# First projection fed from columns of x: one load per pair of k blocks, row statistics behind the key product

## Chip, cores, metric

One core of a Trainium2 chip. The metric is the device time of one execution in microseconds (us), median over runs. One profiled execution stands beside them: its own time, and the span from its first to its last instruction.

## The reference, cut to what matters

Three transformer layers over x (256 rows, 1024 features, float32), each a mixer and a feed-forward net, each behind an rms norm. The change touches the first norm and what is projected from it:

```python
def rmsnorm(x, g):
    y = xf * lax.rsqrt(jnp.mean(xf * xf, axis=-1, keepdims=True) + EPS)
    return (y * g.astype(jnp.float32)).astype(x.dtype)
...
n = rmsnorm(h, g_mix[layer])            # layer 0: h = x
proj = n @ w_in                          # 1024 features -> index queries, keys, q, k, v, gates ...
...
h = h + mixer_ab(n, ...)                 # x again, as rows, for the residual
```

## The kernel before

Every product is made from float32 split into two parts of the fp32r type, "hi" and "lo", as three products: hi·hi, hi·lo, lo·hi. All weights come as one stream of 156 tiles (128 partitions by up to 2048 columns), through three slots of `raw`, `whi`, `wlo` (L450 to L452). SyncE (SP) issues the loads in order, `stage(i)` at L2604; it waits until the lo part of tile i−3 is made. ScalarE (ACT) makes `whi` (`hi`, L1246), VectorE (DVE) makes `wlo` (`lo`, L1864), GpSimd (POOL) does so for parts of a few tiles. All engines run their instructions in the order written out by hand in `tensor_program`, `scalar_program`, `vector_program`, `sync_program`; an instruction that waits holds up all behind it. The eight PSUM banks go round in an order written in `plan_banks` (L269): a product waits until the last user of its bank has read it out.

Start of the kernel. x is loaded as rows, into `h`, in four pieces; between them tile 0 in two pieces (L2617 to L2623), then tiles 1 and 2, constants, the other vectors. TensorE (PE) runs warm-up products (`keep_warm`, L798), turns x by 16 transposes (`half_turn`, L699), and multiplies it with tiles 0 and 1 (`first_proj`, L809: per block k of 128 features and half of the rows three products of 512 columns, 48 in all). ACT reads the transposes out times the gain (`evac_turn`, L1257, hi part), DVE makes the lo part (L1874). The normalising factor of a row is not put in before the products; it is applied when a product is read out. It comes from `row_stats` (L1270): ACT squares the rows and takes exp(−ln/2) of their mean. As a row over all partitions, `RSB`, it is made by two more transposes ("rowf", L846 to L850).

Then, in PE's order: `rowf`, the key product (tile 2, L852 to L856), the first product of tile 3 (L882, "qkb 0") with `key_turn` between its halves, tile 4 ("qkb 1") with `index_turn`, `scores(0, 4)` (L892), and `proj(1)` with tiles 5 and 6. ACT's order behind the first tiles: `row_stats`, hi(2), hi(3), the read-out of the first projection (L1318 to L1321), of `rowf` (L1324), hi(4), hi(5), the keys' read-out (L1327), hi(6). DVE's: lo(2), lo(3), the keys times `RSB` (L1924), lo(4), lo(5), `rope` (L1888), `branch(0)` (L1927), running sums, `level_diff`, lo(6), `branch(1)`, which reads qkb 1 out of its bank. The first bank of `proj(1)` is the one that held qkb 1 (`plan_banks`, by counting).

Of the kernel before, what the change touches and what calls it, by code (L numbers as in the profile page):

```python
# [8 lines left out]
ALU = mybir.AluOpType  # L9
ACT = mybir.ActivationFunctionType  # L10
# [4 lines left out]
P = 128  # L15
# [11 lines left out]
NSLOT = 3  # L27
AHEAD = 2
# [6 lines left out]
    ("gq_row", 128), ("gk_row", 128), ("g_mix0", 8), ("eps", 1),  # L35
# [233 lines left out]
def plan_banks(banks):  # L269
# [135 lines left out]
def block_kernel(nc, W, V, C, DL, CM, TRI, X, MT, WG, GP, OUT):  # L405
    ctx = ExitStack()
    with ctx:
# [98 lines left out]
        o_id = VEC["g_mix0"][0]  # L506
        o_masks = CST["inval"][0]
        GAIN = ["g_mix0", "g_ffn0", "g_mix1", "g_ffn1", "g_mix_pre"]
# [32 lines left out]
        QKE = A(8 * 512).rearrange("p (l n) -> p l n", l=8)  # L541
# [75 lines left out]
        s_w, s_i, s_v, s_c, s_r, s_o, s_g, s_d, s_gp = (sem("s_" + n) for n in ("w", "i", "v", "c", "r", "o", "g", "d", "gp"))  # L617
        s_x = [[sem(f"s_x{tt}{c}") for c in range(2)] for tt in range(2)]
# [7 lines left out]
        s_nhi, s_nlo = sig("nhi", grid(5, 8)), sig("nlo", grid(5, 4))  # L626
        s_un, s_nc, s_nchi, s_nclo = (sig(n, range(4)) for n in ("un", "nc", "nchi", "nclo"))
        s_uhi, s_ulo = sig("uhi", range(8)), sig("ulo", range(8))
        s_stat = sig("stat", grid(5, 3))
# [28 lines left out]
        def n_ready(t, k):  # L658

            if k % 2 == 0:  # L660
                return s_nlo.at(t, k // 2)
            return use["tr", t, k // 2].gone() if t < 4 else s_nodd.at(k // 2)

        def h_ready(t):

            if t == 0:
                return [[(s_x[tt][c], 16) for c in range(2)] for tt in range(2)]
            return [[use["out", t - 1, 2 * tt + c].gone() for c in range(2)] for tt in range(2)]
# [7 lines left out]
        def tensor_program(pe):  # L676
# [128 lines left out]
            keep_warm(use["tr", 0, 2].t, AM[:, 0:P], AM[:, 0:256], 4)  # L805
            half_turn(0, 0)
            keep_warm(use["tr", 0, 2].t, AM[:, 0:P], AM[:, 0:256], 3)

            def first_proj():  # L809
                us = [begin("pj", 0, 0), begin("pj", 0, 1)]  # L810
                w = [weights(i, 4) for i in range(2)]

                def high(k, tt):
                    on.wait_ge(*s_nhi.at(0, k))
                    on.wait_ge(*s_hi01.at(k // 4, k % 4))
                    pe.matmul(us[tt].t[:, :], nTa[:, k, tt * P:tt * P + P].hi, w[k // 4][:, k % 4, :].hi, start=k == 0, stop=False)  # L816

                def low_rows(k, tt):
                    on.wait_ge(*n_ready(0, k))
                    pe.matmul(us[tt].t[:, :], nTa[:, k, tt * P:tt * P + P].lo, w[k // 4][:, k % 4, :].hi, start=False, stop=False)  # L820

                def low_weights(k, tt):
                    weights_in(k // 4, k % 4)
                    return pe.matmul(us[tt].t[:, :], nTa[:, k, tt * P:tt * P + P].hi, w[k // 4][:, k % 4, :].lo, start=False, stop=k == 7)  # L824

                for k, tt in product(range(2), range(2)):
# [24 lines left out]

# [387 lines left out]
        def scalar_program(act):  # L1239
# [30 lines left out]
            def row_stats(t):  # L1270
# [7 lines left out]
                on.wait_ge(*TV)  # L1278
# [581 lines left out]
        def vector_program(dve):  # L1860
# [12 lines left out]

            def evac_turn(t, q, dst):  # L1874
# [47 lines left out]
            on.wait_ge(*use["rowf",].gone())  # L1922
# [677 lines left out]

        def sync_program(sp):
# [132 lines left out]
def vectors(a):  # L2734
# [53 lines left out]
```

## Time and profile before

| | us |
|---|---|
| median of 3 runs | 959.68 |
| lowest, highest | 959.44, 959.92 |
| the profiled execution's own time | 959.49 |
| its span | 957.5 |
| PE busy in the span | 948.9 (99%) |
| DVE, ACT busy | 613.1 (64%), 547.3 (57%) |

A start in the profile is counted from the span's start. Queues of an engine (SPq, ACTq) are its DMA issues. Consecutive like instructions are merged in the timeline: "2.20 ... x4" is four in 2.20 us.

### The profile page before, as it was taken

What the parts mean: (1) busy time and instruction counts of PE and PEld (TensorE: products, weight loads), DVE (VectorE), ACT (ScalarE), POOL (GpSimd) and SP (SyncE); (2) the same over time, 40 slices, a digit from 0 to 9 for tenths busy, and PEclk for the clock granted to TensorE, in tenths of its full rate; (3) what the DMA queues carried; (4) which work ended last, traced back from release to release, by engine and by line L of the source; (5) the groups of instructions that cost most, each with busy time, mean ns of one, the idle gap of its engine ahead of it and who ended that gap; (6) DMA issues with size and microseconds to landing.
All of it is one profiled execution on the core that took longest, in us unless ns stands there. A gap on an engine that the chain in (4) does not pass through costs nothing.

```text
span 957.5 us, 14406 instructions
## 1 busy us (share of the span) xinstructions
PE 948.9 (99%) x5992; PEld 842.8 (88%) x5992; DVE 613.1 (64%) x890; ACT 547.3 (57%) x781; POOL 134.6 (14%) x44
## 2 busy tenths in 40 slices
PE   9999999999999999999999999999999999999997
PEld 7888888888888888888888888899999999999886
DVE  5997847777222667747777522486558699888643
ACT  7676547666333558847666333635465687665442
POOL 0021250000664000020000665300000000000000
PEclk9999999999999999999999999999999999999999
DMA  8554245554555452435544555364444535554541
GB/s 307 214 186 161 90 138 183 204 180 176 201 194 203 156 214 88 177 140 183 204 180 176 196 200 180 140 220 177 156 157 163 185 155 184 207 182 177 187 166 44
DMA packets 25344, 168.21 MB, mean 176 GB/s; under 512 B 2816, under 2 KB 3904, under 8 KB 5568
## 3 DMA queue, kind: packets, MB, share of 16 engines
q1 hardware_dynamic: 25136, 167.23, 48.5%
q8 instruction: 47, 0.77, 0.3%
q14 instruction: 17, 0.14, 0.0%
q10 hardware_dynamic: 144, 0.07, 0.0%
HBM read 166.24 MB, written 1.05 MB: 175 GB/s over the span
## 4 chain that ended last, share of the span: by engine, by line
PE 95%; ACT 2%; DVE 2%; issue 0%; POOL 0%; DVEq 0%; ACTq 0%; POOLq 0%
PE bank L680 23%; PE bank L681 23%; PE bank L682 23%; PE bank L762 12%; PE bank L766 6%; PE bank L708 1%; PE bank L800 1%; DVE wlo L1867 0%; PE bank L900 0%; PE bank L816 0%; PE bank L1030 0%; PE bank L1164 0%; ACT whi L1251 0%; PE bank L824 0%; PE bank L820 0%
## 5 line engine op out<-in xcount | busy, mean ns | idle before, releaser
L1867 DVE TENSOR_TENSOR wlo<-raw,whi 128x2048 fp32r<-128x2048 f32 (+2 forms) x151 | 309.4, 2049 | 249.9 <-ACT whi L1251 249.9
L1251 ACT ACTIVATE whi<-raw 128x2048 fp32r<-128x2048 f32 (+1 forms) x154 | 293.4, 1906 | 151.7 <-PE bank L682 149.9
L2597 POOL TENSOR_TENSOR wlo<-raw,whi 128x1024 fp32r<-128x1024 f32 (+1 forms) x38 | 133.1, 3504 | 473.2 <-ACT whi L1251 465.8
L762 PE MATMUL bank<-nhl,whi 128*128 128x512 f32 x512 | 124.2, 392 | 0.0
L762 PEld LDWEIGHTS bank<-nhl,whi 128*128 128x128 f32 x512 | 93.9, 188 | 19.1 <-issue 0.7
L680 PE MATMUL bank<-mhi,whi 128*128 128x258 f32 x384 | 108.6, 283 | 0.0
L681 PE MATMUL bank<-mlo,whi 128*128 128x258 f32 x384 | 108.3, 282 | 0.0
L682 PE MATMUL bank<-mhi,wlo 128*128 128x258 f32 x384 | 108.2, 282 | 0.0
L680 PE MATMUL bank<-nhl,whi 128*128 128x258 f32 (+3 forms) x320 | 92.3, 288 | 0.8 <-DVE wlo L1867 0.8
L681 PE MATMUL bank<-nhl,whi 128*128 128x258 f32 (+3 forms) x320 | 91.4, 286 | 0.0
L682 PE MATMUL bank<-nhl,wlo 128*128 128x258 f32 (+3 forms) x320 | 90.5, 283 | 0.0
L682 PEld LDWEIGHTS bank<-mhi,wlo 128*128 128x128 f32 x384 | 72.7, 189 | 0.0
L680 PEld LDWEIGHTS bank<-mhi,whi 128*128 128x128 f32 x384 | 72.6, 189 | 0.1
L681 PEld LDWEIGHTS bank<-mlo,whi 128*128 128x128 f32 x384 | 72.6, 189 | 0.0
L680 PE MATMUL bank<-whi,nhl 128*128 128x512 f32 x176 | 70.4, 400 | 0.0
L682 PE MATMUL bank<-whi,nhl 128*128 128x512 f32 x176 | 68.7, 390 | 0.0
L681 PE MATMUL bank<-wlo,nhl 128*128 128x512 f32 x176 | 68.5, 389 | 0.0
L766 PEld LDWEIGHTS bank<-nhl,wlo 128*128 128x128 f32 x512 | 66.2, 191 | 2.5
L766 PE MATMUL bank<-nhl,wlo 128*128 128x256 f32 x512 | 67.7, 283 | 0.0
L680 PEld LDWEIGHTS bank<-nhl,whi 128*128 128x128 f32 (+1 forms) x320 | 60.5, 189 | 1.7 <-DVE wlo L1867 1.0
L681 PEld LDWEIGHTS bank<-nhl,whi 128*128 128x128 f32 (+1 forms) x320 | 60.0, 188 | 0.1
L682 PEld LDWEIGHTS bank<-nhl,wlo 128*128 128x128 f32 (+1 forms) x320 | 60.1, 188 | 0.0
(329 smaller groups left out, 1741.8 us busy)
## 6 DMA issues: line engine op xcount, KB each, us to landing
raw<-w_stream SPq DMA_DIRECT2D x154, 1024.0 KB, 4.8
h<-x_rows SPq DMA_DIRECT2D x4, 256.0 KB, 4.6
raw<-w_stream SPq DMA_DIRECT2D x2, 512.0 KB, 5.6
cst<-consts SPq DMA_DIRECT2D x1, 832.0 KB, 6.4
out_rows<-e SPq DMA_DIRECT2D x3, 256.0 KB, 2.0
e<-g_post SPq DMA_DIRECT2D x1, 512.0 KB, 3.3
raw<-w_stream SPq DMA_DIRECT2D x1, 352.0 KB, 9.1
vec<-vectors SPq DMA_DIRECT2D x1, 258.5 KB, 8.5
```

The lines of the kernel that those rows point to most:

```text
L680: pe.matmul(out, lhsT.hi, rhs.hi, start=start, stop=False)
L681: pe.matmul(out, lhsT.hi, rhs.lo, start=False, stop=False)
L682: return pe.matmul(out, lhsT.lo, rhs.hi, start=False, stop=stop)
L708: x = pe.transpose(u.t[:, kk * 256 + tt * P:kk * 256 + tt * P + P], h[:, tt, k * P:k * P + P], ident)
L762: return pe.matmul(us[c].t[:, :], w[:, k, c * P:c * P + P].hi, nboth[:, k, :], start=k == 0, stop=k == 7)
L766: pe.matmul(us[c].t[:, 0:256], w[:, k, c * P:c * P + P].lo, nTa[:, k, :].hi, start=False, stop=False)
L800: pe.matmul(t[:, 0:256], lhsT, rhs, start=True, stop=True)
L1251: act.activation(whi[j][:, 0:n], raw[j][:, 0:n], ACT.Copy).then_inc(s_hi.up(i))
L1867: dve.tensor_tensor(wlo[j][:, 0:m], raw[j][:, 0:m], whi[j][:, 0:m].bitcast(F32), ALU.subtract).then_inc(s_lod.up(i))
L2597: pool.tensor_tensor(wlo[j][:, m:n], raw[j][:, m:n], whi[j][:, m:n].bitcast(F32), ALU.subtract).then_inc(s_lop.up(i))
```

## The change

Columns of x (features on partitions) come as a new input, `x_cols`, with the first gain as eight columns in front. They are loaded in six parts, each beside the weights of the same k blocks; the first part's weights are issued by ACT, the rest by SP. No transposes of x are made in the first layer; ACT and DVE split the loaded columns directly, and PE's first product runs k by k. The squares are made in place by ACT, summed over k by DVE in three additions, and over partitions by PE with a matrix of ones, behind the key product; from there ACT takes both forms of the factor. The rows of x are loaded before tile 11. The diff is cut to its core.

```diff
+FIRST_PARTS = [(0, 1), (1, 2), (2, 3), (3, 4), (4, 6), (6, 8)]
@@ plan_banks
-    for q in range(4):
-        banks.take("tr", 0, q)
     proj(0)
-    banks.take("rowf")
     banks.take("keys")
     last[KEYS] = (("keys",), 0)
+    banks.take("rowf")
@@ block_kernel
+        xc = qke[:, 0:8 + 8 * S]
+        g_first, XT = xc[:, 0:8], xc[:, 8:8 + 8 * S].rearrange("p (k t) -> p k t", k=8)
+        s_wc = [sem("s_wc0"), sem("s_wc1"), sem("s_wc2"), s_raw[0], sem("s_wc4"), s_raw[1]]
@@ tensor_program
-            keep_warm(use["tr", 0, 2].t, AM[:, 0:P], AM[:, 0:256], 4)
-            half_turn(0, 0)
-            keep_warm(use["tr", 0, 2].t, AM[:, 0:P], AM[:, 0:256], 3)
+            keep_warm(use["rowf",].t, AM[:, 0:P], AM[:, 0:256], 4)
...
-                for k, tt in product(range(2), range(2)):
-                    high(k, tt)
-                half_turn(0, 1)
-                for part in (low_rows, low_weights):
-                    for k, tt in product(range(2), range(2)):
-                        part(k, tt)
-                for k in range(2, 5):
+                for k in range(5):
                     for part in (high, low_rows, low_weights):
                         for tt in range(2):
                             x = part(k, tt)
...
-            u = begin("rowf")
-            on.wait_ge(*s_stat.at(0, 1))
-            for tt in range(2):
-                x = pe.transpose(u.t[:, tt * P:tt * P + P], bc(stats[0][2][:, tt:tt + 1], [P, P]), ident)
-            x.then_inc(u.full)
             w, u = weights(KEYS, 8), begin("keys")
...
+            u = begin("rowf")
+            on.wait_ge(*TC)
+            on.wait_ge(*s_xss.at(2))
+            pe.matmul(u.t[:, 0:256], ones, XT[:, 0, :], start=True, stop=True)
+            for tt in range(2):
+                x = pe.matmul(u.t[:, 256 + tt:257 + tt], XT[:, 0, tt * P:tt * P + P], ones[:, 0:1], start=True, stop=True)
+            x.then_inc(u.full)
             def key_turn():
                 u = begin("keyT")
+                on.wait_ge(*TI)
@@ scalar_program
             def hi01(i, c):
-                on.wait_ge(*((s_w, 16) if i == 0 and c >= 2 else (s_raw[i], 16)))
+                on.wait_ge(s_wc[part_of(4 * i + c)], 16)
...
+            def first_hi(k):
+                on.wait_ge(s_xc[0], 16)
+                on.wait_ge(s_xc[part_of(k)], 16)
+                act.activation(nTa[:, k, :].hi, XT[:, k, :], ACT.Copy, scale=g_first[:, k:k + 1]).then_inc(s_xhi.up(k))
+            def first_squares(j):
+                x = XT[:, 2 * j:2 * j + 2, :]
+                on.wait_ge(*s_xlo.at(2 * j + 1))
+                act.activation(x, x, ACT.Square).then_inc(s_xsq.up(j))
+            def first_stats():
+                ss, lnrs, rs, rs2 = stats[0]
+                u = use["rowf",]
+                on.wait_ge(*TI)
+                on.wait_ge(*u.done())
+                act.activation(ss, u.t[:, 256:258], ACT.Ln, bias=eps, scale=1.0 / D).then_inc(own.up())
+                act.activation(RSB, u.t[:, 0:256], ACT.Ln, bias=eps, scale=1.0 / D).then_inc(u.free)
+                on.wait_ge(*own.last())
+                act.activation(lnrs, ss, ACT.Copy, scale=-0.5).then_inc(s_stat.up(0, 0))
+                act.activation(rs, ss, ACT.Exp, scale=-0.5).then_inc(s_stat.up(0, 1))
+                on.wait_ge(*u.gone())
+                act.activation(RSB, RSB, ACT.Exp, scale=-0.5).then_inc(s_rsb.up(0))
...
-            evac_turn(0, 0, nTa)
-            hi01(0, 0)
-            hi01(0, 1)
-            evac_turn(0, 1, nTa)
...
-            hi01(1, 3)
-            row_stats(0)
-            rs = stats[0][2]
-            on.wait_ge(*s_stat.at(0, 2))
+            for k in range(8):
+                if k:
+                    first_hi(k)
+                hi01(k // 4, k % 4)
+                if k in (4, 5):
+                    first_squares(k - 4)
+            first_squares(2)
+            first_squares(3)
             hi(2)
             hi(3)
+            first_stats()
+            rs = stats[0][2]
+            on.wait_ge(*s_stat.at(0, 1))
             for tt in range(2):
                 u = use["pj", 0, tt]
                 on.wait_ge(*u.done(1))
                 act.activation(IQ[:, tt * 576:tt * 576 + 512], u.t[:, :], ACT.Copy, scale=rs[:, tt:tt + 1]).then_inc(u.free)
-            u = use["rowf",]
-            on.wait_ge(*u.done())
-            act.activation(RSB, u.t[:, 0:256], ACT.Copy).then_inc(u.free)
             hi(4)
             hi(5)
@@ vector_program
+            def first_lo(k):
+                o = nTa[:, k, :]
+                on.wait_ge(*(s_xhi.at(k) if k else s_xhi0.at(0)))
+                dve.scalar_tensor_tensor(out=o.lo, in0=XT[:, k, :], scalar=g_first[:, k:k + 1], in1=o.hi.bitcast(F32),
+                                         op0=ALU.mult, op1=ALU.subtract).then_inc(s_xlo.up(k))
...
-            evac_turn(0, 0, nTa)
-            lo01(0, 0)
-            lo01(0, 1)
-            evac_turn(0, 1, nTa)
...
-            lo01(1, 3)
+            on.wait_ge(s_xc[0], 16)
+            dve.tensor_scalar(nTa[:, 0, :].hi, XT[:, 0, :], g_first[:, 0:1], None, ALU.mult).then_inc(s_xhi0.up(0))
+            for k in range(8):
+                first_lo(k)
+                lo01(k // 4, k % 4)
+            for j, half in enumerate((4, 2, 1)):
+                a = XT[:, 0:half, :]
+                on.wait_ge(*(s_xss.at(j - 1) if j else s_xsq.at(3)))
+                dve.tensor_tensor(a, a, XT[:, half:2 * half, :], ALU.add).then_inc(s_xss.up(j))
             lo(2)
             lo(3)
             u = use["keys",]
-            on.wait_ge(*use["rowf",].gone())
+            on.wait_ge(*s_rsb.at(0))
@@ add_out (residual, first mixer)
+                if s == 0:
+                    on.wait_ge(s_x[tt], 16)
@@ sync_program
+        def first_weights(eng, n):
+            a, b = FIRST_PARTS[n]
+            i, s = a // 4, slice(a % 4 * 512, a % 4 * 512 + (b - a) * 512)
+            src = W[starts[i]:starts[i + 1]].rearrange("(p n) -> p n", p=P)
+            eng.dma_start(raw[i][:, s], src[:, s]).then_inc(s_wc[n], 16)
...
-            first = W[0:starts[1]].rearrange("(p n) -> p n", p=P)
-            for c in range(2):
-                for tt in range(2):
-                    sp.dma_start(h[:, tt, c * 512:c * 512 + 512], X[tt * P:tt * P + P, c * 512:c * 512 + 512]).then_inc(s_x[tt][c], 16)
-                sp.dma_start(raw[0][:, c * 1024:c * 1024 + 1024], first[:, c * 1024:c * 1024 + 1024]).then_inc(s_w if c else s_raw[0], 16)
-            for i in range(1, NSLOT):
-                stage(i)
+            for n, (a, b) in enumerate(FIRST_PARTS):
+                s = slice(8 + a * S if a else 0, 8 + b * S)
+                sp.dma_start(xc[:, s], XC[:, s]).then_inc(s_xc[n], 16)
+                if n:
+                    first_weights(sp, n)
+            sp.dma_start(vec[:, o_id:NVEC], V[:, o_id:NVEC]).then_inc(s_i, 16)
             sp.dma_start(cst[:, 0:o_masks], C[:, 0:o_masks]).then_inc(s_c, 16)
+            stage(2)
+            stage(3)
             sp.dma_start(wg, WG).then_inc(s_c, 16)
             sp.dma_start(vec[:, 0:o_id], V[:, 0:o_id]).then_inc(s_v, 16)
-            for i in range(NSLOT, NTILE):
+            for i in range(NSLOT + 1, NTILE):
+                if i == NSLOT + 8:
+                    for tt in range(2):
+                        sp.dma_start(h[:, tt, :], X[tt * P:tt * P + P, :]).then_inc(s_x[tt], 16)
@@ @block.scalar
-            eng.dma_start(vec[:, o_id:NVEC], V[:, o_id:NVEC]).then_inc(s_i, 16)
+            first_weights(eng, 0)
```

The removed calls of ACT and DVE are those of L1301 to L1312 and L1906 to L1917. `TC` is there when both `cst` and `wg` have landed. The factor exp(−ln) and its wait (L1283, L1289) are left out for the first layer. The constants' layout loses the column block of the first gain.

## Rows read from the trace of the kernel before

**Rows 1.** Page, part 4: shares of the chain that ended last.

```profile
PE 95%; ACT 2%; DVE 2%; issue 0%; POOL 0%; DVEq 0%; ACTq 0%; POOLq 0%
```

**Rows 2.** Waits of PE, whole kernel: us in total, times, longest.

```profile
PE bank L800 <- POOL a L2585: 1.3, 1, 1.3
PE bank L680 <- DVE wlo L1867: 0.8, 1, 0.8
```

**Rows 3.** Timeline of PE: start, us, line, operation, count.

```profile
1.31 3.78 PE L800 MATMUL bank<-a 128*128 128x256 f32 x8 [1.31 <-POOL a L2585]
...
7.49 1.22 PE L816 MATMUL bank<-whi,nhl 128*128 128x512 f32 x4
...
15.36 0.39 PE L816 MATMUL bank<-whi,nhl 128*128 128x512 f32 x1
...
19.21 0.39 PE L824 MATMUL bank<-wlo,nhl 128*128 128x512 f32 x1
...
19.57 0.36 PE L680 MATMUL bank<-nhl,whi 128*88 128x256 f32 x1
...
22.48 0.28 PE L680 MATMUL bank<-nhl,whi 128*128 128x256 f32 x1
...
25.60 1.13 PE L866 MATMUL bank<-a,a 64*128 64x256 f32 x4
...
38.60 0.50 PE L680 MATMUL bank<-whi,nhl 128*128 128x512 f32 x1
```

**Rows 4.** DMA issues at 0.73, 3.06 and 3.53 us: KB, us to landing.

```profile
h<-x_rows SPq DMA_DIRECT2D x1, 256.0 KB, 3.2
raw<-w_stream SPq DMA_DIRECT2D x1, 512.0 KB, 6.4
raw<-w_stream SPq DMA_DIRECT2D x1, 1024.0 KB, 8.5
```

**Rows 5.** Stretches: busy us by engine, granted clock, DMA share, GB/s.

```profile
2.00:3.00 1.00, 1.00 (x4) 0.82 (x3) 0.00 (x0) 0.47 (x1) 0.00 (x0) 1.00 0.70 218
3.00:7.00 4.00, 4.00 (x18) 3.34 (x18) 0.14 (x1) 1.01 (x3) 0.00 (x0) 1.00 0.96 306
8.00:11.00 3.00, 3.00 (x18) 2.60 (x18) 2.45 (x6) 2.20 (x6) 0.00 (x0) 1.00 1.04 433
```

**Rows 6.** Timeline of ACT.

```profile
12.02 2.20 ACT L1255 ACTIVATE whi<-raw 128x512 fp32r<-128x512 f32 x4
...
16.33 0.29 ACT L1279 ACTIVATE rows<-rows,vec 128x2 f32<-128x2 f32 x1
...
17.08 2.60 ACT L1251 ACTIVATE whi<-raw 128x704 fp32r<-128x704 f32 x2
19.58 1.25 ACT L1321 ACTIVATE a<-bank,rows 128x512 f32<-128x512 f32 x2
20.72 0.38 ACT L1324 ACTIVATE a<-bank 128x256 f32<-128x256 f32 x1
20.98 1.92 ACT L1251 ACTIVATE whi<-raw 128x2048 fp32r<-128x2048 f32 x1
...
65.06 1.90 ACT L1251 ACTIVATE whi<-raw 128x2048 fp32r<-128x2048 f32 x1
```

**Rows 7.** Timeline of DVE.

```profile
17.90 0.89 DVE L1867 TENSOR_TENSOR wlo<-raw,whi 128x704 fp32r<-128x704 f32 x1 [2.36 <-ACT whi L1251]
...
26.29 2.29 DVE L1867 TENSOR_TENSOR wlo<-raw,whi 128x2048 fp32r<-128x2048 f32 x1 [0.92 <-ACT whi L1251]
...
33.10 0.42 DVE L1963 TENSOR_TENSOR a<-a 128x256 f32<-128x256 f32 x1
...
36.68 0.69 DVE L1930 SCALAR_TENSOR_TENSOR a<-bank,a 128x512 f32<-128x512 f32 x1
...
50.92 2.28 DVE L1867 TENSOR_TENSOR wlo<-raw,whi 128x2048 fp32r<-128x2048 f32 x1
...
122.97 1.23 DVE L1867 TENSOR_TENSOR wlo<-raw,whi 128x1024 fp32r<-128x1024 f32 x1 [0.39 <-ACT whi L1251]
```

More of the change, by code:

```diff
@@ L34 @@
     ("conv_b_mix", 4), ("g_mix_post", 8), ("g_ffn_pre", 8), ("conv_w_ffn", 132), ("conv_b_ffn", 44),
-    ("gq_row", 128), ("gk_row", 128), ("g_mix0", 8), ("eps", 1),
+    ("gq_row", 128), ("gk_row", 128), ("eps", 1),
     ("ident", 128),
@@ L402, in plan_banks, with block_kernel @@
     return last
-def block_kernel(nc, W, V, C, DL, CM, TRI, X, MT, WG, GP, OUT):
+def block_kernel(nc, W, V, C, DL, CM, TRI, X, XC, MT, WG, GP, OUT):
     ctx = ExitStack()
@@ L505, in block_kernel @@
         ones = const("ones")
-        o_id = VEC["g_mix0"][0]
+        o_id = VEC["eps"][0]
         o_masks = CST["inval"][0]
-        GAIN = ["g_mix0", "g_ffn0", "g_mix1", "g_ffn1", "g_mix_pre"]
+        GAIN = [None, "g_ffn0", "g_mix1", "g_ffn1", "g_mix_pre"]
         stats = [[rows[:, 8 * t + 2 * i:8 * t + 2 * i + 2] for i in range(4)] for t in range(5)]
@@ L540, in block_kernel @@
         QA = xn.rearrange("p t (h d) -> p t h d", h=8)
-        QKE = A(8 * 512).rearrange("p (l n) -> p l n", l=8)
+        qke = A(8 * 512)
+        QKE = qke.rearrange("p (l n) -> p l n", l=8)
+        xc = qke[:, 0:8 + 8 * S]
+        g_first, XT = xc[:, 0:8], xc[:, 8:8 + 8 * S].rearrange("p (k t) -> p k t", k=8)
         IW = small[:, 16:32]
@@ L616, in block_kernel @@
         s_raw = [sem(f"raw{i}") for i in range(NSLOT)]
-        s_w, s_i, s_v, s_c, s_r, s_o, s_g, s_d, s_gp = (sem("s_" + n) for n in ("w", "i", "v", "c", "r", "o", "g", "d", "gp"))
-        s_x = [[sem(f"s_x{tt}{c}") for c in range(2)] for tt in range(2)]
+        s_i, s_v, s_c, s_r, s_o, s_g, s_d, s_gp = (sem("s_" + n) for n in ("i", "v", "c", "r", "o", "g", "d", "gp"))
+        s_x = [sem(f"s_x{tt}") for tt in range(2)]
+        s_xc = [sem(f"s_xc{n}") for n in range(len(FIRST_PARTS))]
+        s_wc = [sem("s_wc0"), sem("s_wc1"), sem("s_wc2"), s_raw[0], sem("s_wc4"), s_raw[1]]
         TI, TV, TC, TR, TM, TD, TGP = (s_i, 16), (s_v, 16), (s_c, 32), (s_r, 32), (s_g, 16), (s_d, 32), (s_gp, 16)
@@ L625, in block_kernel @@
         s_lop = sig("lop", [i for i in range(2, NTILE) if cuts[i] < sizes[i]])
-        s_nhi, s_nlo = sig("nhi", grid(5, 8)), sig("nlo", grid(5, 4))
+        s_xhi0, s_xhi, s_xlo = sig("xhi0", [0]), sig("xhi", range(1, 8)), sig("xlo", range(8))
+        s_nhi, s_nlo = sig("nhi", [(t, k) for t in range(1, 5) for k in range(8)]), sig("nlo", [(t, q) for t in range(1, 5) for q in range(4)])
         s_un, s_nc, s_nchi, s_nclo = (sig(n, range(4)) for n in ("un", "nc", "nchi", "nclo"))
         s_uhi, s_ulo = sig("uhi", range(8)), sig("ulo", range(8))
-        s_stat = sig("stat", grid(5, 3))
+        s_stat = sig("stat", grid(5, 3)[:2] + grid(5, 3)[3:])
+        s_xsq, s_xss = sig("xsq", range(4)), sig("xss", range(3))
         s_dg, s_rsb, s_gl, s_iq, s_key = sig("dg", range(2)), sig("rsb", [0]), sig("gl", [0]), sig("iq", range(2)), sig("key", range(2))
@@ L658, in n_ready @@
         def n_ready(t, k):
+            if t == 0:
+                return s_xlo.at(k)
             if k % 2 == 0:
@@ L662, in n_ready, with part_of @@
             return use["tr", t, k // 2].gone() if t < 4 else s_nodd.at(k // 2)
+        def part_of(k):
+            return next(n for n, (a, b) in enumerate(FIRST_PARTS) if a <= k < b)
         def h_ready(t):
-            if t == 0:
-                return [[(s_x[tt][c], 16) for c in range(2)] for tt in range(2)]
             return [[use["out", t - 1, 2 * tt + c].gone() for c in range(2)] for tt in range(2)]
@@ L813, in high @@
                 def high(k, tt):
-                    on.wait_ge(*s_nhi.at(0, k))
+                    on.wait_ge(*(s_xhi.at(k) if k else s_xhi0.at(0)))
                     on.wait_ge(*s_hi01.at(k // 4, k % 4))
@@ L1253, in hi01 @@
             def hi01(i, c):
-                on.wait_ge(*((s_w, 16) if i == 0 and c >= 2 else (s_raw[i], 16)))
+                on.wait_ge(s_wc[part_of(4 * i + c)], 16)
                 act.activation(whi[i][:, c * 512:c * 512 + 512], raw[i][:, c * 512:c * 512 + 512], ACT.Copy).then_inc(s_hi01.up(i, c))
+            def first_hi(k):
[18 more added lines that the diff above has]
+                act.activation(RSB, RSB, ACT.Exp, scale=-0.5).then_inc(s_rsb.up(0))
             def evac_turn(t, q, dst):
                 u = use["tr", t, q]
-                on.wait_ge(*(TI if t == 0 else TV))
+                on.wait_ge(*TV)
                 on.wait_ge(*u.done())
@@ L1277, in row_stats @@
                 on.wait_ge(*own.last())
-                on.wait_ge(*TV)
+                on.wait_ge(*TI)
                 act.activation(ss, ss, ACT.Ln, bias=eps, scale=1.0 / D).then_inc(own.up())
@@ L1288, in inv_rms_row @@
                 on.wait_ge(*own.last())
-                on.wait_ge(*s_stat.at(t, 2))
                 act.activation(ss, ss, ACT.Exp, bias=stats[t][1][:, tt:tt + 1], scale=-0.5).then_inc(done)
@@ L1872, in lo01 @@
                 dve.tensor_tensor(wlo[i][:, s], raw[i][:, s], whi[i][:, s].bitcast(F32), ALU.subtract).then_inc(s_lo01.up(i, c))
+            def first_lo(k):
+                o = nTa[:, k, :]
+                on.wait_ge(*(s_xhi.at(k) if k else s_xhi0.at(0)))
+                dve.scalar_tensor_tensor(out=o.lo, in0=XT[:, k, :], scalar=g_first[:, k:k + 1], in1=o.hi.bitcast(F32),
+                                         op0=ALU.mult, op1=ALU.subtract).then_inc(s_xlo.up(k))
             def evac_turn(t, q, dst):
@@ L2739, in put @@
         v[:, o:o + n] = np.asarray(x).reshape(-1, P).T
+    put("g_mix1", a["g_mix"][1])
     for l in range(2):
-        put(f"g_mix{l}", a["g_mix"][l])
         put(f"g_ffn{l}", a["g_ffn"][l])
@@ L2769 @@
     c, dlx, cm, tri = constants()
+    x_cols = a["x"][0].T.reshape(8, P, S).transpose(1, 0, 2).reshape(P, 8 * S)
     arrays = {
@@ L2777 @@
         "x_rows": np.ascontiguousarray(a["x"][0]),
+        "x_cols": np.concatenate([a["g_mix"][0].reshape(8, P).T, x_cols], axis=1),
         "meta_cols": np.ascontiguousarray(a["meta_tokens_2"].T.reshape(8, P, META).transpose(1, 0, 2).reshape(P, 8 * META)),
```

14 lines of the change are left out of this document (removed).

## The prediction, made before the changed kernel ran

> **What bounds the kernel now.** I read the shares of the chain first: it is TensorE's work for 95% of the span [rows 1]. The waits say the same: after its start PE waits for nothing longer than 0.8 us [rows 2]. So a microsecond is won or lost only where PE begins, where PE has work taken off it, or where a new wait of PE appears, and what PE loses early no later wait absorbs. The timeline of the start shows the room. PE runs warm-ups from 1.31 us, multiplies the first block at 7.49, reaches tile 3 at 22.48 and `proj(1)` at 38.60 [rows 3]. A 512-column product costs (19.21−15.36)/17 = 0.2265 us there [rows 3]. The last two views are ACT's and DVE's timelines [rows 6, 7]: with the DMA landings [rows 4] they say when what PE needs is ready. This kernel cannot tell less than about 0.2%, 1.9 us, from no change. The profiled execution took 959.49 us, 0.19 below the median; the sum is made against it.
>
> **What the change gives PE.** The warm-ups end at 1.31+3.78 = 5.09 [rows 3]. The first block needs 132 KB of columns and 256 KB of weights, issued together where the first 256 KB of x were, which landed after 3.2 us, at 3.93 [rows 4]; one conversion more (0.55) and products can start behind the warm-ups, 2.4 us earlier than 7.49. The 16 transposes and three of the seven warm-up products go. On PE's path alone tile 3 would start at 5.09 + 48×0.2265 + 2.9 (keys: 22.48−19.57 [rows 3]) + rowf, about 19.9, 2.6 us earlier. That is the whole gain on offer, and it counts only if ACT and DVE are ready too.
>
> **What it puts in their way.** The row statistics were made by ACT while PE multiplied, and waited for no one behind it. Now they are a relay, each step waiting for the one before: squares (ACT), sums over k (DVE), lo(2) queued behind the sums on DVE, key product (PE), rowf (PE), logarithms and exponentials (ACT), and on ACT behind these the read-out of the first projection, hi(4) and hi(5); on DVE lo(4), lo(5), rope and everything to branch(1), whose bank `proj(1)` takes. I follow it step by step.
>
> (a) *Blocks 4 and 5 land.* Ahead of their end are 2308 KB: 6 parts of columns less the last, and tile 0 with half of tile 1. In the trace 2116 KB (vectors, four x pieces, tile 0) had landed at 3.06+6.4 = 9.46 and 3140 KB, with tile 1, at 3.53+8.5 = 12.03 [rows 4]. Read off between the two: 9.95. But tile 1's long rows moved at 433 GB/s from 8 to 11 us, the x and half-tile pieces at 306 from 3 to 7 [rows 5], and the new pieces are all short. With 306 from 7.0 on, the 2.46 us to 9.46 stretch to 3.5 and the last 0.2 MB take 0.65: 11.1. I take 10.3, between these ends, nearer the landings, which are measured.
>
> (b) *ACT, to the last square.* From there ACT runs without a gap: four 256-column conversions (0.38, as the 256-column read-out [rows 6]), four of 512 columns and four squares of 512 (2.20/4 = 0.55 [rows 6]): 1.52 + 4.4 = 5.9. To 16.2.
>
> (c) *DVE.* Three additions over 1024, 512 and 256 columns: 1.23, 0.69, 0.42; then lo(2), 0.89 [rows 7]: 3.2. To 19.4. Tile 2's conversion by ACT falls beside the additions.
>
> (d) *Keys* on PE, 2.9. To 22.3. (e) *rowf*, which the trace does not show. A float32 product of 256 columns takes two passes, 1.13/4 = 0.28 each [rows 3]: 0.56. The two one-column products are four passes, at least nothing and at most 0.28 each: 0.56 to 1.7 in all. I take 1.05, since their streams are short but their weights whole. To 23.35, against 22.48 before: PE's head start is already gone.
>
> (f) *ACT's statistics.* From L1279 to hi(2) was 17.08−16.33 = 0.75, and two 256-column operations come on top at 0.38 [rows 6]: 1.5. (g) First projection read out, 20.72−19.58 = 1.14; (h) hi(4), 1.92 [rows 6]. To 27.9; hi(4) began at 20.98 before, now at 26.0. (i) lo(4) and lo(5), 2.29 each [rows 7]: 32.5 (hi(5), ready at 29.8, is hidden by lo(4)). Before, lo(5) ended at 28.58. (j) From there DVE has no gap to the end of branch(1) at 36.68+0.69 = 37.37 [rows 7], 8.8 later: 41.3. PE stood there at 38.60, that is 1.2 us after the bank was free. Now it waits.
>
> **The sum:** 10.3+5.9+3.2+2.9+1.05+1.5+1.14+1.92+4.58+8.8 = 41.3, against 38.60: +2.7 us, and 959.49+2.7 = 962.2; with the 0.19 to the median, 962.4. With both ends of (a) and (e) the excess is +1.9 to +4.2.
>
> **Edits that I cost at nothing, with their cover.** DVE's first instruction and ACT's first DMA issue lie before 5.09, under the warm-ups. SP issues some fourteen loads before tile 2 and tile 3, at under half a microsecond each; tile 2 is wanted at 16.2. Tile 3's load waits for the fourth block's lo part, some 9.6 us, behind 3.5 MB; at 306 GB/s it lands near 18, lo(3) is done near 22.3 and wanted at 23.35. If that cover goes, each microsecond more delays tile 3 by as much, but not `proj(1)`. The rows of x, 1 MB, now stand before tile 11 on SP: that tile could be asked for from 50.92+2.28 = 53.2 [rows 7] and was converted at 65.06 [rows 6]; one more megabyte fits. Nobody needs these rows before the residual. The new waits on the constants and on the exponential's result are over when asked. The dropped third exponential is on ACT, a tenth of a microsecond.
>
> **Rivals.** *Small parts are slow* (worse). In the microsecond where only x pieces and vectors moved, 2 to 3 us, the rate was 218 GB/s [rows 5], though that was also the ramp. If short rows hold it there, blocks 6 and 7 (3.15 MB to move, 0.22 by 3.0) are moved by 16.4. A landing comes some 0.8 after the last byte: of the 2.17 MB up to 9.46, 1.44 were moved by 7.0 and the rest, at 433, by 8.7 [rows 4, 5]. So 17.2; behind it ACT has 3.0 us to the last square, 20.2, and the relay's remaining 25.1 give 45.3: +6.7, about 966.4. It decides once blocks 6 and 7 land later than 13.2. Against it: the 306 of the next four microseconds, with the same pieces. The Trainium skill ("DMA: Bandwidth & Descriptors", the section Bandwidth) speaks against this change here: it asks for transfers of 1 MiB for three quarters of the peak and gives 138 GB/s for 64 KB ones. By that figure alone the start would be later still, an estimate of over 20 us for the first 3 MB; no row here shows such a rate with several transfers queued.
>
> *The relay is just hidden* (no measurable change). If columns arrive as early as the first x piece did and ACT never waits, its first conversion starts at 3.93 and twelve operations at 0.55 and seven at 0.38 end at 13.2; with 25.1 behind them `proj(1)` starts at 38.3, −0.3 us, 959.4. For it: the DVE additions and the one-column products might be cheaper than my rows. Between this floor and +1.9 all is "no change".
>
> *The head start survives* (faster). PE's own path decides, −2.6 us, 957.1, if lo(5) is done by 27.2, so that branch(1) keeps its 1.2 us ahead of PE; that asks for the last square at 11.1. Against it stands the floor of 13.2 from ACT's rows; for it, that conversions out of the columns may be quicker than those rows, and that nothing in the trace shows the new relay itself.
>
> That the change doesn't do what it says I give no chance of its own: columns are loaded and the transposes are gone in the diff.
>
> **Chances.** Forecast, +1.9 to +4.2: 0.42. Hidden, −0.3 to +1.9: 0.33. Faster: 0.13. Slow parts: 0.12. So faster by over 0.2%: 0.13; within 0.2%: 0.33; slower, forecast and slow parts together: 0.54. The range leaves out the head start and most of the slow parts: from 959.1, the hidden case's floor with a little for its unknown costs, to 964.2, the forecast's upper end with a little of the slow parts. The forecast's own range is 961.6 to 963.9.
>
> **What would show it.** Right: PE's first product near 5.1; a wait of PE for DVE's lo(2) before the keys, of 1 to 2 us; ACT idle before its statistics, hi(4) near 26; a wait of PE at its first `proj(1)` product, which starts near 41.3, with DVE's branch(1) just before it; from there the same distances as before. Wrong: hi(4) before 23, or `proj(1)` at or before 38.6 with no wait in front; landings of blocks 4 and 5 far from 10.3; or a later stage of the kernel that makes up the delay, which would mean that PE was not the bound there.

## The result and the profile after

| | before, us | after, us |
|---|---|---|
| median of the runs timed together | 959.62 | 961.18 |
| lowest, highest | 959.41, 960.09 | 960.64, 961.85 |
| the profiled execution's own time | 959.49 | 961.42 |
| its span | 957.5 | 959.6 |
| first product / tile 3 / `proj(1)` on PE | 7.49 / 22.48 / 38.60 | 5.12 / 23.36 / 40.99 |

One of the changed kernel's 21 runs (1033.48 us, at a granted clock of 0.851 where the others show 0.998 or more) and two of those with lo(2) first below (1795.49 and 2417.11) stand apart and are left out of the lowest, the highest and the ratios; the changed kernel's median without it is 961.16.

The changed kernel is slower: ratio 1.0015, 95% interval 1.0009 to 1.0021, which is +1.56 us or 0.16%. That lies inside the range given (959.1 to 964.2) and 1.2 us under the predicted time. The interval is clear of 1, so these runs tell even 0.16% from no change; the 0.2% that the prediction took as the least that can be told was too coarse. The interval's end only just reaches 0.2%, so "slower by over 0.2%" is not shown: of the three outcomes it is the middle one, to which 0.33 was given.

The shares of the chain that ended last, on the page of the changed kernel:

```profile
PE 92%; DVE 4%; ACT 3%; DMA 1%; issue 1%; SPq 0%; DVEq 0%; ACTq 0%
```

PE's share was 95% [rows 1]. Followed in order of time, the chain before is PE's own from its first warm-up at 1.31 us to `proj(1)`. In the changed kernel it goes through SP's issues (to 4.48), the load of blocks 4 and 5 (to 10.86), ACT (to 16.37), DVE (to 19.62), PE's keys and `rowf`, ACT and DVE again, until `proj(1)` at 40.99. That is where PE's 3%, some 29 us, went. The waits of PE in the changed kernel (engine, line, what it waited for; us in total, times, longest):

```profile
PE bank L690 <- DVE wlo L1886: 1.7, 2, 0.9
PE bank L824 <- ACT whi L1259: 1.7, 3, 1.0
PE bank L810 <- POOL a L2609: 1.3, 1, 1.3
PE bank L690 <- DVE a L1952: 1.0, 1, 1.0
```

Three waits are new against [rows 2]: the first block products wait for conversions, the keys wait for lo(2) (L1886; the other of the two in that row was there before), and one product of line 690 waits for `branch(1)` (L1952 here, L1930 before). PE's timeline in the changed kernel puts them in place (start, us, line, operation, count, idle before):

```profile
5.12 0.70 PE L824 MATMUL bank<-whi,nhl 128*128 128x512 f32 x2 [0.34 <-ACT whi L1259]
...
7.76 0.70 PE L824 MATMUL bank<-whi,nhl 128*128 128x512 f32 x2 [1.01 <-ACT whi L1259]
...
18.33 0.39 PE L832 MATMUL bank<-wlo,nhl 128*128 128x512 f32 x1
19.66 0.35 PE L690 MATMUL bank<-nhl,whi 128*88 128x256 f32 x1 [0.94 <-DVE wlo L1886]
...
22.56 0.60 PE L856 MATMUL bank<-a,cst 128*128 128x256 f32 x2
22.99 0.50 PE L858 MATMUL bank<-cst,a 128*128 128x1 f32 x4
23.36 0.36 PE L690 MATMUL bank<-nhl,whi 128*128 128x256 f32 x1
...
40.99 0.50 PE L690 MATMUL bank<-whi,nhl 128*128 128x512 f32 x1 [1.03 <-DVE a L1952]
```

Read it beside [rows 3]. PE starts 2.4 us earlier. Its last product of the first projection starts 0.9 earlier (18.33 against 19.21). Tile 3 starts 0.9 later, after the wait for lo(2) and the new `rowf`. `proj(1)` starts 2.39 later, behind a wait of 1.03. The place where the time goes is the stretch between, on ACT and DVE. ACT in the changed kernel:

```profile
9.63 0.51 ACT L1264 ACTIVATE nhl<-a 128x256 fp32r<-128x256 f32 x1
10.88 0.63 ACT L1259 ACTIVATE whi<-raw 128x512 fp32r<-128x512 f32 x1 [0.74 <-DMA raw<-w_stream]
...
15.22 1.14 ACT L1269 ACTIVATE a<-a 128x512 f32<-128x512 f32 x2
...
23.59 0.26 ACT L1276 ACTIVATE rows<-bank,vec 128x2 f32<-128x2 f32 x1 [4.37 <-PE bank L858]
...
24.60 1.26 ACT L1343 ACTIVATE a<-bank,rows 128x512 f32<-128x512 f32 x2
25.74 3.73 ACT L1255 ACTIVATE whi<-raw 128x2048 fp32r<-128x2048 f32 x2
```

and DVE:

```profile
16.39 2.41 DVE L1939 TENSOR_TENSOR a<-a 128x1024 f32<-128x1024 f32 x3 [0.27 <-ACT a L1269]
18.72 3.08 DVE L1886 TENSOR_TENSOR wlo<-raw,whi 128x704 fp32r<-128x704 f32 x2
...
27.70 4.49 DVE L1886 TENSOR_TENSOR wlo<-raw,whi 128x2048 fp32r<-128x2048 f32 x2 [2.54 <-ACT whi L1255]
...
38.05 2.28 DVE L1886 TENSOR_TENSOR wlo<-raw,whi 128x2048 fp32r<-128x2048 f32 x1
40.25 0.68 DVE L1952 SCALAR_TENSOR_TENSOR a<-bank,a 128x512 f32<-128x512 f32 x1
```

ACT stands idle for 4.37 us in front of the statistics, with hi(4) queued behind them; hi(4) starts at 25.74 where it started at 20.98 [rows 6]. DVE then stands idle for 2.54 us in front of lo(4), and frees the bank of `proj(1)` with `branch(1)` at 40.93.

From there the kernel runs as before: span less the start of `proj(1)` is 957.5−38.60 = 918.9 before and 959.6−40.99 = 918.6 after. The delay is still the same 2.39 far into the kernel, before and after:

```profile
618.72 0.60 PE L1109 MATMUL bank<-vec,rows 128*128 128x128 f32 x4
621.11 0.60 PE L1113 MATMUL bank<-vec,rows 128*128 128x128 f32 x4
```

Some 0.3 us of it came back between 716 and 734 us, in a stretch of products without a wait between them. The experiments below have the same order of work from `proj(1)` on and run 918.7 to 918.9, so I take the 0.3 for scatter between executions.

### The profile page after: what moved, and what is told of

Its sections match the earlier page's. It is cut to its first block, busy times and chain, and to the rows that moved or that the text cites. A ratio compares the mean times of both kernels' runs of the same rounds, so it can differ in the third digit from the quotient of the medians.

```text
span 959.6 us, 14382 instructions
## 1 busy us (share of the span) xinstructions
PE 947.3 (99%) x5974; PEld 839.8 (88%) x5974; DVE 616.0 (64%) x894; ACT 547.3 (57%) x780; POOL 135.8 (14%) x44
## 3 DMA queue, kind: packets, MB, share of 16 engines
HBM read 167.29 MB, written 1.05 MB: 175 GB/s over the span
## 4 chain that ended last, share of the span: by engine, by line
PE 92%; DVE 4%; ACT 3%; DMA 1%; issue 1%; SPq 0%; DVEq 0%; ACTq 0%
PE bank L690 23%; PE bank L691 22%; PE bank L692 22%; PE bank L772 12%; PE bank L776 6%; DVE wlo L1886 1%; PE bank L718 1%; DMA raw<-w_stream 1%; ACT whi L1255 1%; PE bank L1034 0%; PE bank L1168 0%; PE bank L1060 0%; PE bank L1042 0%; PE bank L940 0%; DVE e L2590 0%
## 5 line engine op out<-in xcount | busy, mean ns | idle before, releaser
L1886 DVE TENSOR_TENSOR wlo<-raw,whi 128x2048 fp32r<-128x2048 f32 (+2 forms) x151 | 307.0, 2035 | 247.6 <-ACT whi L1255 247.6
```

Source lines behind the costliest of these rows:

```text
L1886: dve.tensor_tensor(wlo[j][:, 0:m], raw[j][:, 0:m], whi[j][:, 0:m].bitcast(F32), ALU.subtract).then_inc(s_lod.up(i))
```

## The experiments

Each is an edit of the changed kernel. The times beside them are medians of 9 to 11 runs, against 959.76 or 959.77 for the kernel before on the same chip; the changed kernel stood at +1.56. "Block 4" is the start of ACT's conversion of its weights. In the six-part kernels ACT waited for them, so that is when they had landed; with eight parts ACT hardly waited, and they had landed by then.

| kernel | block 4 | statistics (ACT) | hi(4) | tile 3 | `proj(1)` | PE's wait there | span | median | ratio, 95% interval |
|---|---|---|---|---|---|---|---|---|---|
| before | – | – | 20.98 | 22.48 | 38.60 | none | 957.5 | 959.62 | |
| after | 10.88 | 23.59 | 25.74 | 23.36 | 40.99 | 1.03 | 959.6 | 961.18 | 1.0015 (1.0009 to 1.0021) |
| hi(4) first | 10.21 | 22.90 | 20.20 | 22.66 | 38.85 | none | 957.6 | 960.13 | 1.0005 (0.9995 to 1.0014) |
| lo(2) first | 10.27 | 21.82 | 23.97 | 21.92 | 39.22 | 1.01 | 957.9 | 959.89 | 1.0003 (0.9993 to 1.0012) |
| both | 10.23 | 22.04 | 20.22 | 21.89 | 38.10 | none | 956.8 | 959.00 | 0.9992 (0.9984 to 1.0001) |
| eight parts | 9.38 | 22.09 | 24.24 | 21.85 | 39.49 | 1.03 | 958.4 | 960.14 | 1.0004 (0.9995 to 1.0013) |
| seven warm-ups | 10.17 | 22.86 | 25.01 | 22.62 | 40.26 | 1.04 | 959.0 | 960.94 | 1.0013 (1.0004 to 1.0022) |
| no squares | 10.79 | 21.74 | 23.89 | 21.51 | 39.14 | 1.02 | 958.0 | 959.34 | 0.9995 (0.9986 to 1.0004) |
| all moves, squares on POOL | 9.38 | 22.18 | 20.36 | 21.61 | 37.81 | none | 956.5 | 958.85 | 0.9993 (0.9984 to 1.0001) |
| rows of x later | 10.56 | 23.27 | 25.42 | 23.03 | 40.66 | 1.03 | 959.5 | 961.00 | 1.0013 (1.0004 to 1.0022) |

The theory is the relay of the prediction: squares, sums, lo(2), keys, `rowf`, statistics, read-out, hi(4), lo(4), lo(5), DVE's list, `branch(1)`. If it holds, each step taken off it moves `proj(1)` by as much, until PE's own path decides. A single profile carries its own landing of block 4, so shifts along the relay are best read from "block 4" on. From there to `proj(1)` it is 30.11 us in the changed kernel, and 30.11, 30.09 and 30.10 with eight parts, seven warm-ups and the later rows, which leave the relay behind block 4 as it was. It is 28.64, 28.95 and 28.35 with hi(4) first, lo(2) first and no squares.

The worth of an edit is taken from the medians: its distance to the kernel before on its own chip, less the changed kernel's 1.56. For hi(4) first, lo(2) first and eight parts the interval still overlaps the changed kernel's (1.0009 to 1.0021), so there the medians alone don't decide and the profiles are needed; for both orders, no squares and all moves it does not overlap.

### hi(4) ahead of the statistics

```diff
             hi(3)
+            hi(4)
             first_stats()
...
-            hi(4)
             hi(5)
```

> hi(4) on ACT moved ahead of the statistics, where ACT waits 4.4 us for rowf. Relay theory: hi(4) starts when tile 4 lands, near 21, instead of 25.7; lo(4) follows the keys' scaling near 25.2, lo(5) ends near 30.0 instead of 32.2, and proj(1) starts 1.0 to 2.2 us earlier than in the changed kernel (41.0), at 38.8 to 40; the time falls by as much, to about 959.5 to 960.2. Rival, the landing of the small parts is all that costs: hi(4)'s place is then of no consequence, the time stays within 0.4 us of the changed kernel (961.2).

ACT and PE in this kernel:

```profile
20.20 1.92 ACT L1255 ACTIVATE whi<-raw 128x2048 fp32r<-128x2048 f32 x1 [2.01 <-DMA raw<-w_stream]
```

```profile
38.85 0.50 PE L690 MATMUL bank<-whi,nhl 128*128 128x512 f32 x1
```

Only ACT's queue order has changed. The idle time in front of the statistics (4.37) now holds hi(4), which is limited by tile 4's landing; rope starts at 29.22 instead of 32.11; and the wait in front of `proj(1)` is gone. By the medians it is worth 1.2 us (+0.37 in place of +1.56). From block 4 to `proj(1)` it is 1.5 shorter. So the second half of the relay was on the path only because hi(4) stood behind the statistics. What PE still loses here is its wait of 0.92 for lo(2) and the products of `rowf`.

### lo(2) ahead of the sums

```diff
                 lo01(k // 4, k % 4)
+            lo(2)
             for j, half in enumerate((4, 2, 1)):
...
             rs = stats[0][2]
-            lo(2)
             lo(3)
```

> lo(2) on DVE moved ahead of the three sums. Relay theory: lo(2) is done near 18 instead of 19.6, the keys follow the first projection without PE's 0.9 us wait, rowf ends 0.9 us earlier and everything behind it, proj(1) included, is 0.9 us earlier: about 960.3. Rival, the relay is bound by the sums themselves: rowf then waits for them as long as the keys did before, and the time stays at 961.2.

DVE and PE in this kernel:

```profile
16.46 0.89 DVE L1886 TENSOR_TENSOR wlo<-raw,whi 128x704 fp32r<-128x704 f32 x1 [0.95 <-ACT whi L1255]
17.27 2.40 DVE L1940 TENSOR_TENSOR a<-a 128x1024 f32<-128x1024 f32 x3
```

```profile
17.96 0.28 PE L690 MATMUL bank<-nhl,whi 128*88 128x256 f32 x1
...
39.22 0.50 PE L690 MATMUL bank<-whi,nhl 128*128 128x512 f32 x1 [1.01 <-DVE a L1952]
```

The keys now start at 17.96, right behind the last product of the first projection, and run beside the sums instead of after them. Of the 1.77 by which hi(4) moves, 0.61 is the earlier landing and 1.2 the edit; the medians say 1.4 (+0.13 in place of +1.56). Both are more than the 0.9 expected. The relay still sets `proj(1)`: the wait of 1.01 stays, and so does the distance from rope to `proj(1)`, 8.88 after and 8.89 here, which is DVE's list without a gap.

### Both orders

The two edits together.

> Both moves at once. Relay theory: hi(4) near 21, rowf near 22.4, statistics behind hi(4) near 23, lo(5) done near 29.3, proj(1) at 38.3 to 39.0, PE without a wait of 0.5 us or more in front of it: about 959.0 to 959.6, level with the kernel before or up to 0.5 us under it. Rival (landing): 961 as before.

```profile
38.10 0.50 PE L690 MATMUL bank<-whi,nhl 128*128 128x512 f32 x1
```

Here PE sets `proj(1)`: from tile 3 it is 38.10−21.89 = 16.21, as before the change (38.60−22.48 = 16.12). By the medians the two edits are worth 2.3 us, and the kernel is 0.76 below the one before; the interval against the latter ends at 1.0001. So with both orders changed the columns cost nothing and may be worth some 0.8 us, and both losses came from the order of instructions. Of PE's early start of 2.4 us only 0.6 is left at tile 3: the keys start at 17.92, 1.65 ahead of [rows 3], and `rowf` with a short wait for lo(3) (0.21) takes 1.0 of that back.

### Eight parts in place of six

```diff
-FIRST_PARTS = [(0, 1), (1, 2), (2, 3), (3, 4), (4, 6), (6, 8)]
+FIRST_PARTS = [(k, k + 1) for k in range(8)]
...
```

> Columns and weights in eight parts, one for each k block, instead of six. Relay theory: the chain starts where block 4 lands; alone, its weights are half as long, it lands near 10 instead of 10.9, and the last square comes about 0.6 us earlier, unless blocks 6 and 7 now land later than 13.2: 960.4 to 961.0. Rival (small parts are slow): two more issues and shorter rows cost, blocks 4 to 7 land later, the time rises by 0.5 us or more, to 961.7 and above.

This is the test of the rival "small parts are slow". In the changed kernel the first four parts hold one block each already and only the last two hold a pair (the title's "one load per pair" is true of those two alone); here the pairs are split as well. Stretches of the changed kernel first (busy us by engine with counts, granted clock, DMA share, GB/s), then the same two here:

```profile
3.00:7.00 4.00, 3.41 (x11) 2.15 (x10) 1.91 (x4) 1.04 (x3) 0.00 (x0) 1.00 0.95 289
7.00:11.00 4.00, 3.24 (x14) 2.74 (x15) 3.09 (x6) 3.23 (x7) 0.00 (x0) 1.00 1.01 362
```

```profile
3.00:7.00 4.00, 3.87 (x12) 2.43 (x12) 2.35 (x5) 2.06 (x4) 0.00 (x0) 1.00 0.98 320
7.00:11.00 4.00, 4.00 (x19) 3.31 (x18) 3.50 (x8) 3.68 (x8) 0.00 (x0) 1.00 1.06 373
```

```profile
9.38 0.63 ACT L1259 ACTIVATE whi<-raw 128x512 fp32r<-128x512 f32 x1
...
39.49 0.50 PE L690 MATMUL bank<-whi,nhl 128*128 128x512 f32 x1 [1.03 <-DVE a L1952]
```

Parts of 128 and 256 KB were moved no slower than parts of 256 and 512 KB. That they were moved faster is not shown: the seven profiled six-part kernels have 272 to 297 GB/s in the first stretch and 330 to 415 in the second. Each part can be used as soon as it is there: block 4 is converted at 9.38 instead of 10.2 to 10.9, the sums start at 14.89 instead of 16.39, and the medians fall by 1.2 us (+0.38 in place of +1.56). That is more than I had expected of it.

### Seven warm-up products, as before

```diff
-            keep_warm(use["rowf",].t, AM[:, 0:P], AM[:, 0:256], 4)
+            keep_warm(use["rowf",].t, AM[:, 0:P], AM[:, 0:256], 7)
```

> The changed kernel with its three warm-up products back, all seven ahead of the first product. Relay theory: PE has time to spare until the keys; the first product starts 0.5 to 0.9 us later than 5.1 but block 1 is waited for as before, and the time stays within 0.4 us of the changed kernel (961.2). Rival, PE's own start sets the time: 0.5 to 0.9 us later throughout, 961.7 to 962.1.

PE here:

```profile
1.31 6.16 PE L810 MATMUL bank<-a 128*128 128x256 f32 x14 [1.31 <-POOL a L2609]
7.09 0.84 PE L824 MATMUL bank<-whi,nhl 128*128 128x512 f32 x2
...
40.26 0.50 PE L690 MATMUL bank<-whi,nhl 128*128 128x512 f32 x1 [1.04 <-DVE a L1952]
```

PE's first product is 2.0 us later, where 0.5 to 0.9 was expected, and the time still does not rise (+1.17 in place of +1.56, with overlapping intervals). In the changed kernel as it stands, PE's early start is worth nothing.

### Without the squares and sums

```diff
-                if k in (4, 5):
-                    first_squares(k - 4)
-            first_squares(2)
-            first_squares(3)
...
-            for j, half in enumerate((4, 2, 1)):
...
-            on.wait_ge(*s_xss.at(2))
-            pe.matmul(u.t[:, 0:256], ones, XT[:, 0, :], start=True, stop=True)
+            pe.matmul(u.t[:, 0:256], ones, AM[:, 0:256], start=True, stop=True)
...
```

The squares and their sums over k are left out, and `rowf` and the statistics are made from zeros; every other step stays.

> Leaves out the squares on ACT and the three sums on DVE; rowf and the statistics are made from zeros at the same place. Relay theory: lo(2) is done 3 us earlier, the keys follow the first projection at 17 to 17.5, rowf ends near 21, lo(5) near 30 and proj(1) starts 1.8 to 2.6 us earlier than in the changed kernel: 958.7 to 959.5. Rival (landing of the parts alone): squares and sums lie beside it, 960.8 or more.

ACT and PE here:

```profile
21.74 0.26 ACT L1275 ACTIVATE rows<-bank,vec 128x2 f32<-128x2 f32 x1 [2.62 <-PE bank L857]
```

```profile
39.14 0.50 PE L690 MATMUL bank<-whi,nhl 128*128 128x512 f32 x1 [1.02 <-DVE a L1943]
```

Squares and sums cost 2.0 us by the medians (−0.43 in place of +1.56), and 1.8 by the profiles (hi(4) at 23.89 in place of 25.74, of which 0.09 is the landing). `proj(1)` still waits 1.02 for DVE, so even free statistics would leave the relay's second half in place.

With lo(2) first the statistics start at nearly the same time (21.82) and so does hi(4) (23.97): in both kernels PE runs keys and `rowf` without a wait behind the first projection, and that sets ACT. But this profile has the later landing, by 0.52. Read from block 4 on, the way to `proj(1)` is 0.6 shorter here, and the median is 0.6 lower too. So with lo(2) moved ahead squares and sums may still cost up to some 0.6 us; the spreads overlap, and this was not followed up.

### All moves, eight parts, squares on POOL

Both orders and the eight parts, and in place of ACT's squares:

```diff
+            for j in range(4):
+                x = XT[:, 2 * j:2 * j + 2, :]
+                on.wait_ge(*s_xlo.at(2 * j + 1))
+                pool.tensor_tensor(x, x, x, ALU.mult).then_inc(s_xsq.up(j))
```

> Both moves, eight parts, and the squares on GpSimd, which is idle there, instead of ACT. Relay theory: the last square comes from GpSimd about 1.2 us after the last low part, near 15.5, the sums are done before the keys are, tile 3's landing (17.3) and lo(3) near 21.3 set PE; proj(1) at 37.2 to 37.8 against 38.6 before the change: 958.2 to 958.9, about 1 us under the kernel before. Rival: GpSimd's squares are slow beside DVE (over 2 us each), the sums come later than the keys and the gain over both moves alone (959.0) is nil or negative.

POOL, DVE, ACT and PE here:

```profile
14.85 1.43 POOL L2609 TENSOR_TENSOR a<-a 128x512 f32<-128x512 f32 x1 [1.36 <-DVE nhl L1892]
```

```profile
15.30 1.73 DVE L1882 TENSOR_TENSOR wlo<-raw,whi 128x704 fp32r<-128x704 f32 x1
```

```profile
16.67 1.92 ACT L1255 ACTIVATE whi<-raw 128x2048 fp32r<-128x2048 f32 x1 [2.03 <-DMA raw<-w_stream]
```

```profile
37.81 0.50 PE L690 MATMUL bank<-whi,nhl 128*128 128x512 f32 x1
```

`proj(1)` is earliest of all, 0.8 us before [rows 3], and the median, 958.85, is the lowest, 0.9 under the kernel before; the interval (0.9984 to 1.0001) just touches no change. Against both orders alone it is 0.15, within the scatter. ACT now waits for tiles 3 and 4 to land (2.03 and 1.76), so what POOL takes off ACT turns into waiting. And POOL's squares lengthen DVE's work: lo(2), which starts beside the last of them, takes 1.73 where it takes 0.89 with lo(2) first, and the last square ends at 16.28, where 15.5 was expected.

### The rows of x before tile 14

```diff
-                if i == NSLOT + 8:
+                if i == NSLOT + 11:
```

> The rows of x are loaded before tile 14 instead of tile 11. Both theories: nobody waits for them before the residual near 140 us, and tile 11 has 7 us to spare; the time stays within 0.4 us of the changed kernel (961.2). If the late megabyte was part of the loss, the time moves by more than that.

```profile
40.66 0.50 PE L690 MATMUL bank<-whi,nhl 128*128 128x512 f32 x1 [1.03 <-DVE a L1952]
```

961.00 against 961.18, and 959.5−40.66 = 918.8 from `proj(1)` on: the megabyte of rows costs nothing where the change put it.

## Why the prediction was right, and where it was not

**The relay.** Each step of the sum as it was put, beside the profile of the changed kernel (the next step's start less its own; (i) runs to the end of lo(5), 27.70+4.49, and (j) from there):

| step | predicted | measured | from, to |
|---|---|---|---|
| (a) blocks 4 and 5 land | 10.3 | 10.88 | ACT's conversion of block 4 |
| (b) ACT, to the last square | 5.9 | 5.51 | 10.88, 16.39 |
| (c) sums, lo(2) | 3.2 | 3.27 | 16.39, 19.66 |
| (d) keys | 2.9 | 2.90 | 19.66, 22.56 |
| (e) `rowf` | 1.05 | 1.03 | 22.56, 23.59 |
| (f) statistics | 1.5 | 1.01 | 23.59, 24.60 |
| (g) read-out | 1.14 | 1.14 | 24.60, 25.74 |
| (h) hi(4) | 1.92 | 1.96 | 25.74, 27.70 |
| (i) lo(4), lo(5) | 4.58 | 4.49 | 27.70, 32.19 |
| (j) to `proj(1)` | 8.8 | 8.80 | 32.19, 40.99 |
| sum | 41.3 | 40.99 | |

The mechanism is shown: taking hi(4) off the relay removes the wait, taking lo(2) or the squares off shortens it, an earlier landing shortens it, and PE's early start (seven warm-ups) and the rows of x have no part in it. The signs named came, one of them a little smaller and the landing 0.6 late: the first product at 5.12, PE's wait for lo(2) (0.94, where 1 to 2 was expected), ACT idle before its statistics, hi(4) at 25.74, a wait at `proj(1)` behind `branch(1)`, and the same distances from there.

**The size.** Two terms were too long. In (b) four 256-column conversions were counted from the landing on; there were three, since block 4's columns were there before its weights and ACT converted them at 9.63, in the time it had to wait for those. One such conversion takes 0.40 from start to start, which is all of the 0.39; the distances between the 512-column operations, 0.52 to 0.54 against the 0.55 assumed, and between the others, 0.40 against 0.38, cancel nearly. In (f) the small instructions were put in with the whole 0.75 of [rows 6], to which they come with the instruction that is dropped, 0.22 there to the next start, and with a wait of the second for the first: 0.32 from the logarithm to the next. ACT in the kernel before, behind the logarithm at 16.33:

```profile
16.65 0.20 ACT L1281 ACTIVATE rows<-rows 128x2 f32<-128x2 f32 x1
...
16.86 0.19 ACT L1283 ACTIVATE rows<-rows 128x2 f32<-128x2 f32 x1
```

The changed kernel drops the last of these, the exponential at 16.86, and its second, 256-column logarithm runs in that wait. ACT's starts there:

```profile
23.75 0.47 ACT L1277 ACTIVATE a<-bank,vec 128x256 f32<-128x256 f32 x1
24.11 0.20 ACT L1279 ACTIVATE rows<-rows 128x2 f32<-128x2 f32 x1
24.20 0.20 ACT L1280 ACTIVATE rows<-rows 128x2 f32<-128x2 f32 x1
24.29 0.41 ACT L1282 ACTIVATE a<-a 128x256 f32<-128x256 f32 x1
```

From start to start the small ones now take 0.16, 0.09 and 0.09, the two long ones 0.36 and 0.31: 1.01. Against that, (a) was 0.6 too early in this execution. The six-part kernels have 10.17 to 10.88 for it, so 10.3 is within what the landings do, and this profile is of a late one.

From the predicted 962.4 to the median 961.18 the difference is thus 1.2: 0.3 is the sum; 0.3 is the stretch from `proj(1)` to the end, which was shorter in this execution; 0.2 is what lies around the span (1.82 after, 1.99 before); and 0.4 is the step from a profiled execution to the median, 0.19 upwards as predicted and 0.24 downwards in fact, which is what its late landing would give; that this is the cause is not shown. With the landing near the early end of its scatter the relay of 30.1 would give `proj(1)` at 40.3, as the seven warm-ups show (40.26), +1.7.

**The chances.** 0.54 went to more than 0.2% and the time came out at 0.16%. That is no failure of the mechanism: the lower end of the forecast was +1.9, the terms that came out shorter, (b) and (f), had been given no ends of their own, and the band between 0 and +1.9 was called "hidden", though a relay that is not hidden can end there as it did. The bounds should have taken in ACT's terms too.

**The rivals.** *Small parts are slow* would have decided once blocks 6 and 7 landed later than 13.2. They landed at 13.0, issued at 5.43:

```profile
raw<-w_stream SPq DMA_DIRECT2D x1, 512.0 KB, 7.6
```

and ACT, with its squares in between, had not to wait for them. That is only 0.2 under the limit. The rates were 289 and 362 GB/s, and eight smaller parts were no slower. What the Trainium skill ("DMA: Bandwidth & Descriptors", the section Bandwidth) states for a transfer of 64 KB, 138 GB/s, was measured there on transfers issued by GpSimd, and is not what several parts of 128 to 512 KB queued by SP got here; for these the measurement decides, and 3 MB did not take the 20 us estimated from that page. *The relay is just hidden* falls as a mechanism: PE waits for DVE. *The head start survives* needed lo(5) done by 27.2; it was done at 32.19. (The prediction's own terms give 10.9 for the last square there, not 11.1, and `branch(1)` would then end just as PE arrives; to keep its lead of 1.2 us as well, lo(5) would have to be done by 26.0.) It came nearest in the two kernels with both orders changed, where PE's own path decides, and even there only 0.5 (both orders) and 0.8 (all moves) of the 2.6 remained at `proj(1)`.

**Where PE's head start went.** The 48 products of the first projection take from 5.12 to 18.33 and one more distance, 13.4 us, where PE alone needs 48×0.2265 = 10.9: of the 2.6 more, 1.3 are the two listed waits for ACT's conversions inside it (1.01 and 0.31), and the rest are products that start late block by block. That was in the prediction only as "if ACT and DVE are ready too" and not as a term, because the relay made it void.

## What to carry to other kernels

Where a change moves a quantity behind a new step, follow every engine's queue from there and ask what stands *behind* the waiting instruction that needs none of it: one line's order on ACT (hi(4) ahead of the statistics) and one on DVE (lo(2) ahead of the sums) were worth some 1 us each, and together turned a loss of 1.6 us into a gain of some 0.8, which the interval only just fails to tell from none. The same pattern stands a third time in the changed kernel: `branch(1)` needs the last product of qkb 1, which starts at 37.64, and stands on DVE behind lo(6), which starts at 38.05 and takes 2.28. Whether putting it ahead of lo(6) removes PE's last wait was not tried. A head start on the bounding engine is worth only what is left of it where that engine next meets the others. And when a sum is made of instructions queued on one engine, use the distances between starts and ask of each what fills its wait: an instruction that needs nothing can run in it, as the second logarithm and block 4's conversion did here.

## What the runs showed of the hardware that was not expected

The same opening loads of the six-part kernel, to the end of blocks 4 and 5, land at 10.17 to 10.88 us over seven profiled executions, and the changed kernel, with them on its path, spreads over 960.64 to 961.85, where the kernel before spreads over 959.41 to 960.09. What sets the landing was not found. Block 1's weights (256 KB, issued at 1.64 by SP) took 5.3 us to land, though block 1's columns, issued a little before on the same queue, took 3.5; this is PE's wait of 1.01 at 7.76; in the other runs no wait of these products is over 0.45. POOL's square of 128x512 took 1.43 us where DVE worked beside it (the first of the four, with DVE less busy, 1.04), and DVE paid too: a low part of 128x256 that started beside such a square took 1.26 us where it takes 0.47 otherwise.
